# The experts' activations turned on VectorE instead of TensorE, and attention two's reciprocals spread straight from their columns

## The reference, cut to what matters

```python
for g in range(N_GROUPS):                       # 4 groups of 4 experts, D = 1024, F = 512
    h = silu(einsum('nd,edf->nef', xt, w_gate[e])) * einsum('nd,edf->nef', xt, w_up[e])
    h = h * combine[:, g, :, None]
    y = y + einsum('nef,efd->nd', h, w_down[e])
```

```python
p = softmax(concatenate([s_loc, s_ctx], -1))    # 8 heads of 64
o = p[..., :n_loc] @ v_rows + p[..., n_loc:] @ vc
```

## Time and profile before

| what | value |
|---|---|
| median of 3 runs | 901.18 us |
| the profiled execution's own time | 901.18 us |
| its span, first to last instruction | 899.4 us |
| TensorE matmul busy | 887.7 us, 99% |
| VectorE busy | 386.4 us, 43% |
| ScalarE busy | 213.6 us, 24% |
| GpSimd busy | 172.2 us, 19% |
| granted TensorE clock | 1.000 |
| HBM read and written | 168.70 and 16.79 MB |
| chain of waits | PE 90%, DVE 3%, DMA 2%, ACT 2% |

### The profile page before, as it was taken

One profiled execution on the slowest core, in us unless ns is written; L12 is line 12 of the kernel. 1 busy time (PEld: TensorE's weight loads), 2 busy tenths in 40 slices (PEclk: granted clock), 3 DMA queues, 4 the chain that ended last, 5 costly groups with the idle time before them and its releaser, 6 DMA issues.

```text
span 899.4 us, 13457 instructions
## 1 busy us (share of the span) xinstructions
PE 887.7 (99%) x5562; PEld 502.7 (56%) x5562; DVE 386.4 (43%) x814; ACT 213.6 (24%) x468; POOL 172.2 (19%) x160
## 2 busy tenths in 40 slices
PE   9999999999999989999999999999999999999998
PEld 5588875455565543333333333344688888866553
DVE  2764543357764346310310310048635542354456
ACT  2211213345544310010110110115201111643420
POOL 3212220000002044140230200033201303191000
PEclk9999999999999999999999999999999999999999
DMA  9945559124010738999999999961382102700002
GB/s 329 326 113 188 188 181 391 60 94 188 1 47 9 271 125 331 405 413 429 423 420 428 420 430 426 401 239 47 110 163 96 51 24 68 249 11 1 2 1 93
DMA packets 54830, 184.28 MB, mean 205 GB/s; under 512 B 15049, under 2 KB 15717, under 8 KB 48497
## 3 DMA queue, kind: packets, MB, share of 16 engines
q1 hardware_dynamic: 46368, 162.41, 48.0%
q0 software_dynamic: 4912, 14.18, 4.3%
q10 hardware_dynamic: 3488, 6.82, 2.0%
HBM read 168.70 MB, written 16.79 MB: 206 GB/s over the span
## 4 chain that ended last, share of the span: by engine, by line
PE 90%; DVE 3%; DMA 2%; ACT 2%; POOL 1%; issue 1%; SPq 0%; DVEq 0%; ACTq 0%; POOLq 0%
PE psum L981 20%; PE psum L1185 18%; PE psum L1206 9%; PE psum L1083 6%; PE psum L885 6%; PE psum L1031 4%; PE psum L1008 4%; PE psum L1457 3%; PE psum L1337 2%; PE psum L1299 2%; PE psum L1045 2%; PE psum L1062 2%; PE psum L1406 2%; PE psum L1110 2%; PE psum L944 1%
## 5 line engine op out<-in xcount | busy, mean ns | idle before, releaser
L1185 PE MATMUL psum<-ring,buf_a 128*32 128x512 f32 x1536 | 166.4, 592 | 1.6 <-issue 1.6
L1185 PEld LDWEIGHTS psum<-ring,buf_a 128*32 128x32 f32 x1536 | 51.6, 110 | 112.8 <-issue 112.8
L1206 PE MATMUL psum<-ring,buf_c 128*32 128x512 f32 x768 | 84.1, 593 | 0.0
L2718 POOL DMA_INDIRECT buf_b<-xq_d,o_sb x48 | 52.6, 1096 | 157.5 <-DVE buf_a L2300 125.1
L2649 POOL TENSOR_TENSOR qk_st<-qk_st,half 128x8 f32<-128x8 f32 x26 | 43.6, 1677 | 160.2 <-DVE qk_st L2384 74.5
L2325 DVE TENSOR_TENSOR buf_c<-buf_c,psum 128x512 f32<-128x512 f32 x12 | 13.1, 1093 | 141.0 <-PE psum L1185 141.0
L981 PE MATMUL psum<-ring,buf_a 128*128 128x256 f32 x320 | 70.9, 380 | 0.0
L981 PE MATMUL psum<-ring,buf_b 128*128 128x256 f32 x288 | 64.8, 380 | 0.0
L981 PEld LDWEIGHTS psum<-ring,buf_a 128*128 128x128 f32 x320 | 60.1, 190 | 8.2 <-issue 0.4
L1948 DVE TENSOR_TENSOR s_buf<-s_buf,psum 128x512 f32<-128x512 f32 x52 | 35.3, 685 | 61.2 <-PE psum L981 58.7
L981 PEld LDWEIGHTS psum<-ring,buf_b 128*128 128x128 f32 x288 | 53.9, 190 | 7.5 <-issue 0.6
(11 more groups left out here) (319 smaller groups left out, 1229.9 us busy)
## 6 DMA issues: line engine op xcount, KB each, us to landing
ring<-in_moe_w_gate SPq DMA_DIRECT2D x16, 2048.0 KB, 13.7
ring<-in_moe_w_up SPq DMA_DIRECT2D x16, 2048.0 KB, 14.8
ring<-in_moe_w_down SPq DMA_DIRECT2D x16, 2048.0 KB, 13.9
ring<-in_w_in SPq DMA_DIRECT2D x7, 2048.0 KB, 12.5
ring<-in_w_ada SPq DMA_DIRECT2D x6, 2048.0 KB, 9.8
ring<-in_da_w_in SPq DMA_DIRECT2D x5, 2048.0 KB, 14.4
y_d<-ring POOLq DMA_DIRECT2D x1, 5632.0 KB, 22.0
y_d<-buf_b ACTq DMA_DIRECT2D x11, 512.0 KB, 11.5
```

The source lines that it names most:

```text
L1185: last = mm(buf("mm", n)[rows, :], x_part[:, j, k, :], slot(moe_load(q, m, r))[:, k, :], start=(k == 0), stop=(k == KD - 1))
L1206: last = mm(buf("sc", n)[rows, m, :], hidT[:, s % 3, f * P + SUB * j:f * P + SUB * (j + 1)], slot(moe_load(q, 2, r), FC)[:, f, m * CH:(m + ...
L2718: pool.indirect_dma_start(out=xg[:, s % 2, j * 256:(j + 1) * 256], out_offset=None, in_=xn_quarters, in_offset=bass.IndirectOffsetOnAxis(a ...
```

## The change

- `hid_transposes` and its step `hid` go, on TensorE and on ScalarE, with their turns at the `tp` banks. The rest of the order stays: `up b`, `up c`, `down a`, `down b`, `down c`.
- VectorE writes the product of `sg` and the up pass in 16 pieces of 32 rows by 128 columns: the piece of sub-tile j and columns 128 to goes to the quadrant `to` of `hid` (32 partitions), at columns 128j, with column 4a + k of the piece at place 32k + a. Both inputs are read four floats apart, the output is contiguous. It then waits for its own writes and turns `hid` in 32x32 blocks into `hidT`, one `transpose` of 128x512, and counts `hid_turned`. From the fourth set on the turn waits for the down pass of three sets before.
- `down` waits for `hid_turned` and takes its weights from the new places. GpSimd waits for the last `hid_turned` before it gathers the result rows.
- In attention two the diagonal goes. `spread` makes eight products instead of two; the weights of each are one column of `rden`, read 64 times (a step of zero), and the moving side is the identity. `diag` is the reciprocal alone.

The branch for overflowing rows is left as it is, but for one wait.

```diff
@@ moe_steps()
-        todo += [("up", b), ("hid", a), ("up", c)]
-        todo += [("hid", b), ("down", a)]
+        todo += [("up", b), ("up", c), ("down", a)]
         if q == 0:
             todo.append(("last_T", 0))
-        todo += [("hid", c), ("down", b)]
+        todo.append(("down", b))
@@ TensorE
-        def hid_transposes(s):
-            drained(pe, "mm", turn["mm", "up", s])
-            n = turn["tp", "hid", s]
-            claim(pe, "tp", n)
-            transposes(n, [hid[:, s % 2, g * P:(g + 1) * P] for g in range(FC)])
-
         def down(s):
             n = turn["sc", "down", s]
             claim(pe, "sc", n)
-            drained(pe, "tp", turn["tp", "hid", s])
+            pe.wait_ge(hid_turned, s + 1)
...
-                        last = mm(buf("sc", n)[rows, m, :], hidT[:, s % 3, f * P + SUB * j:f * P + SUB * (j + 1)],
+                        last = mm(buf("sc", n)[rows, m, :], hidT[:, s % 3, (FC * j + f) * SUB:(FC * j + f + 1) * SUB],
                                   slot(moe_load(q, 2, r), FC)[:, f, m * CH:(m + 1) * CH],
                                   start=(f == 0), stop=(f == FC - 1))
@@ TensorE, spread
-                    for hh in range(2):
-                        last = mm(buf("tp", n)[hh * DH:(hh + 1) * DH, :], ones[:, 0:DH],
-                                  o_sb[:, hh * 512:(hh + 1) * 512], start=True, stop=True)
+                    for g in range(4):
+                        for hh in range(2):
+                            last = mm(buf("tp", n)[hh * DH:(hh + 1) * DH, g * P:(g + 1) * P],
+                                      rden[:, m % 2, 2 * g + hh:2 * g + hh + 1].to_broadcast([P, DH]), ident[:], start=True, stop=True)
@@ ScalarE
-            elif name == "hid":
-                n = turn["tp", "hid", s]
-                filled(act, "tp", n)
-                drain(S.copy(hidT[:, s % 3, :], buf("tp", n)), "tp", n)
@@ VectorE, up
-                if s >= 2:
-                    filled(dve, "tp", turn["tp", "hid", s - 2])
-                drain(V.tensor_tensor(hid[:, s % 2, :].rearrange("p (k q) -> p q k", k=FC), by_row(sg[:, s % 3, :]),
-                                      by_row(buf("mm", n)), ALU.mult), "mm", n)
+                for j in range(4):
+                    rows = slice(SUB * j, SUB * (j + 1))
+                    for to in range(4):
+                        columns = slice(to * P, (to + 1) * P)
+                        last = V.tensor_tensor(
+                            hid[SUB * to:SUB * (to + 1), s % 2, j * P:(j + 1) * P].rearrange("p (k a) -> p k a", k=FC),
+                            sg[rows, s % 3, columns].rearrange("p (a k) -> p k a", k=FC),
+                            buf("mm", n)[rows, columns].rearrange("p (a k) -> p k a", k=FC), ALU.mult)
+                drain(last, "mm", n)
+                drained(dve, "mm", n)
+                if s >= 3:
+                    filled(dve, "sc", turn["sc", "down", s - 3])
+                V.transpose(hidT[:, s % 3, :], hid[:, s % 2, :]).then_inc(hid_turned, 1)
@@ VectorE, diag
-                    link(V.reciprocal(rden[:, m % 2, :], rden[:, m % 2, :]))
-                    if m > 0:
-                        dve.wait_ge(mix_ready, m)
-                    V.tensor_tensor(rden_diag, ident[:].unsqueeze(1).unsqueeze(1).to_broadcast([P, 2, 4, P]),
-                                    rden[:, m % 2, :].rearrange("p (g h) -> p h g", h=2).unsqueeze(3).to_broadcast([P, 2, 4, P]),
-                                    ALU.mult).then_inc(rden_ready, 1)
+                    V.reciprocal(rden[:, m % 2, :], rden[:, m % 2, :]).then_inc(rden_ready, 1)
@@ GpSimd, before the result rows
+        pool.wait_ge(hid_turned, SETS)
```

More of the change, by code:

```diff
@@ L388, in build @@
     gate_diag = o_sb[:].rearrange("p (k n) -> p k n", k=KD)
-    rden_diag = o_sb[:].rearrange("p (h g n) -> p h g n", h=2, g=4)
     q2T = buf_c[:, 0:2048].rearrange("p (g n) -> p g n", g=4)
@@ L503, in build @@
             book("mm", name, m)
-        elif name == "hid":
-            book("tp", "hid", m)
         elif name == "down":
@@ L630, in build @@
     ids_zeroed, ids_stored = sem("ids_zeroed"), sem("ids_stored")
+    hid_turned = sem("hid_turned")
     x_turned, x_ready, xq_stored = sem("x_turned"), sem("x_ready"), sem("xq_stored")
@@ L1215, in _ @@
                 gate_or_up(1, s)
-            elif name == "hid":
-                hid_transposes(s)
             elif name == "down":
```

## The result

The changed kernel takes **904.90 us** (median of 5, 903.75 to 906.38) against 901.18 (901.07 to 902.05). The ratio is 1.0040, with a 95% interval of 1.0025 to 1.0054: slower, by more than the 0.2% that can be told from nothing, and above the forecast's range (896.8 to 903.2). The profiled execution is the fastest of the five, 903.75 us with a span of 902.0, so 2.6 of the 3.7 us can be followed in it.

A forecast was written before the change was run, and what follows sets the result against it. TensorE was taken to bound the expert stage by a hair, the weight stream right behind. Experts -0.4, behind them +0.5 and attention two -1.0 gave -0.9 against 901.18: 900.3 us, range 896.8 to 903.2.

The forecast's parts named there:

- VectorE's new work: Experts: 16 multiplies of 0.39 us, 6.2 us a set, plus a 0.71 us transpose; covered from the second quarter on.
- The stall at `gate 2`: First quarter of the experts: x_turn(2) queues behind the multiplies on VectorE, so TensorE stands for 3.6 us.
- What the stall does to the weights: Two `down` loads leave 3.6 us later; the full weight stream shifts by 2.8 us (bounds 1.5 and 3.6).
- critical load: Second `up` load of the experts' last quarter: landed at 545.2 before with 1.0 us reserve, forecast to land at 548.0.
- The experts: Expert stage: ends at 589.1 instead of 589.5, 0.4 us earlier, not the 5.0 of TensorE's own sum.
- Behind the experts: Last store and gathers after the expert stage: perhaps 0.5 us longer (0 to 1.5) beside the later weight stream.
- Attention two: Diagonal's visible wait of 0.45 us goes and four spreads get 0.15 us shorter each: together -1.0 us.
- Rival 2: Weight stream in the experts is no bound, so all of 5.0 + 1.0 comes through: 895.2 us; chance 0.1.
- Rival 3: VectorE too slow at `gate 2` and at `up c`'s bank claim, 0.53 us a multiply: 903.1 us; chance 0.17.

The follow-up runs named there:

- e1: The change with x_turn(2) moved ahead of up 0's multiplies in VectorE's queue; 899.50 us, ratio 0.9983.
- e4: The change with 17 unused products of ones on TensorE before its wait for x_turn(2) at gate 2; 902.40 us, ratio 1.0019.
- e7: The change with both multiply inputs read in step and the output written in step, quadrants as in the change; 902.26 us, ratio 1.0008.
- e6: The change with the 16 multiplies writing to the quadrant they read from; 901.29 us, ratio 1.0003.
- e3: The change without its part in attention two; 905.71 us, ratio 1.0048.
- e5: e1 with each w_down load cut to its first half (1 MB of 2 MB); 893.32 us, ratio 0.9915.
- e8: The kernel before with nine dependent multiplies on unused rows ahead of x_turn(2) on VectorE, so gate 2 waits as in the change; 907.88 us, ratio 1.0071.
- e9: e1 with five weight loads of the first quarter each issued in two halves, the first half earlier; 899.35 us, ratio 0.9979.
- e10: e1 run once more, beside e9 on one chip; 899.23 us, ratio 0.9983.
- e11: e1 with unused products of ones on TensorE before three passes that wait for weights in the third and fourth quarters; 899.58 us, ratio 0.9980.

## Why the prediction was wrong

The mechanism was right in each place that the forecast names, but one was missing, the fall of the clock. The term of its sum that failed is what the stall at `gate 2` does to the weights, and two smaller ones were off.

- **VectorE's new work**: 386 ns and 0.40 apart, 6.4 us a set, and 0.71 for the transpose, against 0.39, 6.2 and 0.71. Right. It is covered in the later quarters, as forecast: no `up` pass waits for a bank.
- **The stall at `gate 2`**: 3.6 forecast, 3.63 measured. Right, and e1 shows that it starts everything.
- **What the stall does to the weights**, the step that failed: "The full stream shifts by 2.8 us (bounds 1.5 and 3.6)". It shifted by 5.2, for two reasons. First, the pass behind the stall was taken at its old length; with 3.6 us idle in front of it the clock fell, and the slots came free 1.9 us later again (e4). Second, I let 0.8 us of the delay be hidden behind the lone load under way. Nothing of the kind is there: in the change the second of the two loads, issued 5.5 us late at 365.3, takes 12.2 us instead of 12.1. How late the two loads leave, and how late the critical load lands, each against before, from the profiles:

| kernel | idle at `gate 2` | clock dips | two loads leave later by | critical load lands | later by | experts end |
|---|---|---|---|---|---|---|
| before | 0 | no | - | 545.2 | - | 589.5 |
| e1 | 0 | no | 0 | 545.0 | -0.2 | 586.5 |
| e7 | 2.0 | no | 2.1 | 546.8 | 1.6 | 588.3 |
| e4 | 0 (kept busy) | no | 4.2 | 549.0 | 3.8 | 590.5 |
| e6 | 2.6 | yes | 4.3 | 549.0 | 3.8 | 590.5 |
| change | 3.6 | yes | 5.5 | 550.4 | 5.2 | 591.9 |
| e3 | 3.6 | yes | 6.7 | 551.6 | 6.4 | 593.0 |

  The delays (the first of the two loads against 359.4, when it left before) come out again one to one, less 0.3 to 0.5 us.
- **The experts**: from the pass that waits for the critical load to the end it is 41.3 us in every kernel of the table but the first, forecast 41.1 from the landing (0.14 earlier). With 5.2 in place of 2.8 the forecast's own formula gives 545.2 + 5.2 + 41.1 = 591.5, and 591.9 was measured.
- **Behind the experts**, +0.5 forecast: from their end to the first scores of attention two it is 178.14 us in the change (591.88 to 770.02) and 177.45 before (589.53 to 766.98): +0.7. Of this 0.58 is the new wait for VectorE at 606.5. The last store takes 6.75 instead of 6.17 us, as forecast.
- **Attention two**: -1.0 forecast. From its first scores to the first spread it is 24.10 us in the change (to 794.12) and 24.63 before (to 791.61), and the rest is as long as before: -0.5 in the profile. The wait went, the spread didn't get shorter.
- The sum in the profile: +2.4 for the experts, +0.7, -0.5, together +2.6, as measured. The other 1.1 us of the median are not shown by a trace of the change. The other executions have a granted clock of 0.996 (three) or 0.998, and e3's profile, one of 0.996, lost 2.9 us to the dip where the change's lost 1.9; a longer dip would account for it.

Rival 2 (the stream is no bound) is refuted by e5 against e1. Rival 3 named the right place and sign, but a price of the multiplies that they don't have; at 0.40 each it should not have turned the sign. The largest cost that turned it is one that none of the rivals had, the clock. The stream's unhidden delay and the attention's smaller gain did the rest: e4, without the dip, is still 0.2% slower than before. The trace of before could not show the clock's fall; it has the clock at 1.00 throughout and no idle time of this length in the stage.

Not settled: why the same stall is followed by 1.9 us of loss in one execution and by 3.0 in another. In e3 and e8 the clock is down already before `gate 2` starts (0.75 and 0.79 between 354 and 356 us) and until about 362, in the change it isn't down before 356 and is back at 1.00 from 360 on. Nor why 2.55 us of idle time brought it down in e6 and 2.92 in e1 didn't; and how much more than e1 an earlier stream would bring, which e9 didn't test cleanly.

## What to carry to other kernels

Before a stage's second engine is loaded with more work, look at what stands behind that work in its own queue: here 5.7 us hung on two lines' order, while the 65 us of added VectorE time, once out of the way, held TensorE for 0.24 us at most in the profiles of e1, e10 and e11. An idle gap on TensorE is to be priced with the slower passes behind it and with the transfers that those passes release, not at its own length. And where a stage's weight stream runs at a share of 1.0, time taken off TensorE is worth only the reserve with which the weights land, and what is saved behind the last load that binds: of the 8.6 us that the experts lost in work, e1 kept 3.0.

## What the runs showed of the hardware

- 3.6 us of idle time in a TensorE that was busy until then was followed by the clock's lower level for most of 4 us (0.58 and 0.54 in windows of 2 us), and for over 6 us in e8 after 3.8; 17 small products in the same gap kept it at 1.00. The clock was down behind 2.55 us of idle time in e6's profile, and stayed up behind 2.04 in e7's and 2.92 in e1's.
- A 32x128 multiply on VectorE lasts 284 ns in step and 386 ns with a 16-byte step in both inputs, one of them in PSUM: the 0.80 ns an element are paid once, not per input. To another quadrant multiplies with the step start 0.40 us apart, within a quadrant 0.31.
- A TensorE weight load that reads one column 64 times (a step of zero) takes 132 to 137 ns, the same as one of 64 columns.
